# Five expert loads of each layer, asked for in three transfers of 8, 8 and 112 rows

## The reference, cut to what matters

```python
for l in range(DEPTH):                      # DEPTH = 2
    mix = _token_mixer(x, w_in[l], ..., w_out[l])
    x = _layer_norm(ALPHA * x + mix, ln1_g[l], ln1_b[l])
    ffn = _moe(x, w_router[l], b_router[l], w_gate[l], w_up[l], w_down[l], ws_gate[l], ws_up[l], ws_down[l])
    x = _layer_norm(ALPHA * x + ffn, ln2_g[l], ln2_b[l])

def expert_rows(args):                      # one of 64 experts, width 256
    xb, e = args
    h = jax.nn.silu(xb @ w_gate[e]) * (xb @ w_up[e])
    return h @ w_down[e]
```

## Time and profile before

| what | value |
|---|---|
| median of 3 runs | 1236.44 us (1235.01 to 1237.77) |
| the profiled execution, its own time | 1237.52 us |
| span of its trace, first to last instruction | 1235.7 us |
| PE busy | 1209.2 us, 98% |
| DVE, ACT, POOL busy | 560.4, 343.6, 123.8 us |
| granted clock of TensorE, mean | 0.994 |
| moved by DMA | 454.88 MB, mean 368 GB/s |

### The profile page before, as it was taken

The page is one execution under the profiler, slowest core; times in us unless marked ns, Lnnn a source line. Parts: engine busy times, 40 slices in busy tenths (PEclk is TensorE's granted clock), DMA queues, the critical chain, the costliest instruction groups (busy, mean ns, idle before and its releaser), DMA issues.

```text
span 1235.7 us, 25287 instructions
## 1 busy us (share of the span) xinstructions
PE 1209.2 (98%) x10417; PEld 631.1 (51%) x10417; DVE 560.4 (45%) x1552; ACT 343.6 (28%) x703; POOL 123.8 (10%) x173
## 2 busy tenths in 40 slices
PE   9999999999999999999999999999999999999996
PEld 8886753344344343433389868434433444443342
DVE  6888653333333333333378877433333333333334
ACT  5657411111111111111266574111111111111111
POOL 2662100000000000000035522000000000000000
PEclk9999999999999999999999999999999999999998
DMA  9554799999999999999845539999999999999994
GB/s 361 180 187 182 301 405 427 424 427 425 427 424 424 429 425 427 425 427 426 342 170 203 201 141 360 412 427 426 424 429 426 425 425 427 428 425 426 424 428 200
DMA packets 42425, 454.88 MB, mean 368 GB/s; under 512 B 4944, under 2 KB 5712, under 8 KB 8016
## 3 DMA queue, kind: packets, MB, share of 16 engines
q1 hardware_dynamic: 42032, 452.27, 88.0%
q10 hardware_dynamic: 288, 1.05, 0.2%
HBM read 452.26 MB, written 1.05 MB: 367 GB/s over the span
## 4 chain that ended last, share of the span: by engine, by line
PE 83%; DVE 9%; DMA 5%; ACT 2%; issue 1%; POOL 1%; DVEq 0%; ACTq 0%; POOLq 0%
PE banks L1078 34%; PE banks L1098 17%; PE banks L1054 7%; PE banks L1109 5%; DMA expert_weights<-in_moe_w 5%; PE banks L1086 2%; PE banks L610 1%; PE banks L998 1%; PE banks L612 1%; PE banks L611 1%; PE banks L947 1%; PE banks L1035 1%; PE banks L949 1%; PE banks L948 1%; DVE prob L1719 1%
## 5 line engine op out<-in xcount | busy, mean ns | idle before, releaser
L1078 PE MATMUL banks<-expert_weights,gathered 128*64 128x512 f32 x1520 | 341.5, 598 | 2.4 <-DMA expert_weights<-in_moe_w 2.4
L1078 PEld LDWEIGHTS banks<-expert_weights,gathered 128*64 128x64 f32 x1520 | 106.0, 137 | 232.9 <-issue 232.9
L1098 PE MATMUL banks<-expert_weights,hT 128*32 128x512 f32 x1600 | 182.0, 595 | 2.5 <-DVE hT L1926 2.5
L1921 DVE TENSOR_TENSOR sig<-sig,banks 128x256 f32<-128x256 f32 x64 | 27.0, 421 | 339.8 <-ACT sig L1451 339.5
L1464 ACT ACTIVATE y_hi<-banks,gate_slot 128x512 fp32r<-128x512 f32 x126 | 86.6, 687 | 295.1 <-PE banks L1098 295.1
L1931 DVE SCALAR_TENSOR_TENSOR y_lo<-banks,gate_slot,y_hi 128x512 fp32r<-128x512 f32 x126 | 94.7, 751 | 157.6 <-ACT y_hi L1464 157.6
L1451 ACT ACTIVATE sig<-banks 128x256 f32<-128x256 f32 x64 | 24.6, 384 | 410.5 <-PE banks L1078 410.5
L1054 PEld LDWEIGHTS banks<-hot,x_part 128*128 128x128 bf16 x3072 | 93.3, 98 | 48.7 <-issue 48.7
L1098 PEld LDWEIGHTS banks<-expert_weights,hT 128*32 128x32 f32 x1600 | 47.5, 109 | 109.4 <-issue 107.9
L1054 PE MATMUL banks<-hot,x_part 128*128 128x64 bf16 x3072 | 100.6, 193 | 0.0
L1520 POOL TENSOR_TENSOR piece_lo<-pieces,piece_hi 128x256 fp32r<-128x256 f32 x112 | 88.7, 828 | 75.3 <-ACT piece_hi L1275 61.0
(11 more groups left out here) (250 smaller groups left out, 1530.9 us busy)
## 6 DMA issues: line engine op xcount, KB each, us to landing
expert_weights<-in_moe_w SPq DMA_DIRECT2D x132, 2048.0 KB, 23.4
expert_weights_in_ring<-in_moe_w SPq DMA_DIRECT2D x20, 2048.0 KB, 23.4
pieces<-in_pieces SPq DMA_DIRECT2D x32, 1024.0 KB, 5.9
expert_weights<-in_moe_w SPq DMA_DIRECT2D x26, 1024.0 KB, 9.3
expert_weights_in_rows<-in_moe_w SPq DMA_DIRECT2D x22, 1024.0 KB, 22.5
expert_weights_in_x<-in_moe_w SPq DMA_DIRECT2D x22, 1024.0 KB, 23.3
expert_weights_in_ring<-in_moe_w SPq DMA_DIRECT2D x8, 1024.0 KB, 8.9
shared_weights<-in_ws SPq DMA_DIRECT2D x2, 3072.0 KB, 12.2
```

Source lines behind the costliest of these rows:

```text
L1078: mm = pe.matmul(C[e * PAIR:(e + 1) * PAIR, :], xgT[:, d, e * PAIR:(e + 1) * PAIR], w[e][:, part], start=(d == 0), stop=(d == KD - 1))
L1098: mm = pe.matmul((A, B)[c][to:to + SLOTS, :], hT[:, f, of_:of_ + SLOTS], W[QUARTERS + c][e][:, f * 512:(f + 1) * 512], start=(f == 0), sto ...
```

## The change

Five loads of each layer, k = 20, 36, 52, 68 and 84, are asked for in three transfers in place of one: rows 0 to 7, rows 8 to 15, and rows 16 to 127. All go into the same room, and each adds 16 to the room's semaphore, so that the counts for which PE waits take them in. All five are loads of room 4 (`expert_weights`), and none is in `IN_TWO`. What is read and where it is stored is unchanged, and no wait is added.

```diff
+LOW_ENGINES = 8
+IN_ROWS = [k for k in range(20, LOADS * PAIRS, 16)]
+assert not [k for k in IN_ROWS if k in IN_TWO]
+def rows_of(k):
+    if k not in IN_ROWS:
+        return [slice(0, P)]
+    return [slice(0, LOW_ENGINES), slice(LOW_ENGINES, 2 * LOW_ENGINES), slice(2 * LOW_ENGINES, P)]
...
-        room_ld = [sem(f"weights_loaded{r}", 16 * sum(room_of(k) == r for k in range(1, LOADS * PAIRS))) for r in range(ROOMS)]
+        room_ld = [sem(f"weights_loaded{r}", 16 * sum(len(rows_of(k)) for k in range(1, LOADS * PAIRS) if room_of(k) == r)) for r in range(ROOMS)]
...
-                return room_ld[room_of(k)], 16 * sum(room_of(m) == room_of(k) for m in before)
+                return room_ld[room_of(k)], 16 * sum(len(rows_of(m)) for m in before if room_of(m) == room_of(k))
...
                     def load(k):
-                        sp.dma_start(rooms[room_of(k)].rearrange("p j e c -> p (j e c)"), of(moe_w)[0, k // LOADS, k % LOADS]).then_inc(room_ld[room_of(k)], 16)
+                        for rows_ in rows_of(k):
+                            sp.dma_start(rooms[room_of(k)][rows_].rearrange("p j e c -> p (j e c)"), of(moe_w)[0, k // LOADS, k % LOADS, rows_]).then_inc(room_ld[room_of(k)], 16)
```

## The result

The changed kernel takes 1334.45 us (median of 4, 1329.41 to 1353.33) where the kernel before takes 1236.87 us (median of 4). The ratio is 1.0781, with a 95% interval of 1.0759 to 1.0802. I had forecast 1232.5 us, range 1231.0 to 1243.5: 98 us lost where 4 were to be won.

The account below looks back on a forecast made before the run. PE and DMA were taken to end nearly together, PE waiting only for the last pair's load; 2.06 + 1.68 + 0.33 = 4.07 us off 1236.44 gave 1232.4, put as 1232.5 us, range 1231.0 to 1243.5.

Parts of the forecast that it names:

- What bounds the kernel: PE and DMA end nearly together; PE waits only for load 94, the last pair's second gate/up half, 2.4 us in all.
- Step 1, the balance: Over five loads a layer, eight engines move 9 rows and eight 7 per load: 3.08 us more and 3.08 us less.
- The upper bound I set for the unknown form: If all eight rows of an 8-row transfer went to one engine, it would get 46 us more in a layer.
- The rule that the prediction used: On the load queue, 8-row transfers take engines 0 to 7 and the 112 rows take all 16.
- Step 2, which half is late: At a layer's end eight engines are late by 6.0 us; about two in three that the change loads the early half.
- Rival A: Late engines, or even one, take the 8-row transfers; load 94 lands 3.08 us later: 1242.6 to 1244.3 us; chance 0.26.
- The evidence I leaned on: At `in_first`, first packets start 0.95 us after issue, with late engines busy or all 16 free; called weak.
- Step 3, what PE gains: At the last pair, waits of 2.06 and 0.33 us and a clock loss of 1.68 us go: 4.07 us in sum.
- Steps 4 and 5, SP and semaphores: Ten more SP issues a layer, 0.33 to 0.40 us each, cost nothing; the extra semaphore increments take no PE time.
- B: The 8-row transfers spread over all 16 engines, so nothing shifts and PE waits as before: 1236.4 us; chance 0.07.
- C: Only part of the gain at PE's last-pair waits comes, 2.06 us or less: 1234.4 to 1236 us; chance 0.07.
- my slower rival: Rival A: late engines get extra rows, load 94 lands later in each layer, up to 1244.3 us; chance 0.26.

Follow-up runs that it names:

- slabs of 8-row transfers: Form tried against the kernel before: some columns of a load go in 16 transfers of 8 rows in steps of 4, the rest in one of 128; 1244.8 to 1267.4 us.
- the run with five slabs: Against the kernel before, all five loads send columns 0 to 511 in 16 transfers of 8 rows in steps of 4, the rest whole; 1267.4 us, ratio 1.0245.
- the two sides crossed: Against the kernel before: HBM read even/odd, SBUF written in halves side by side, 1329.8 us, 1.0758; HBM read in halves, SBUF written even/odd, 1236.1 us, 0.9999.
- one slab: Against the kernel before, load 84 alone sends columns 0 to 1279 in 16 transfers of 8 rows in steps of 4, the rest whole; 1244.8 us, ratio 1.0062.
- (two): Against the kernel before, loads 68 and 84 send columns 0 to 1279 in 16 transfers of 8 rows in steps of 4, the rest whole; 1256.3 us, 1.0153.

## Why the prediction was wrong, point by point

**What bounds the kernel.** Right. With the queues relieved of 43 us of work (the run with only rows 0 to 15) PE waits for no transfer.

**Step 1, the balance, is where it failed.** I priced a row at 0.615 us, "at 426/16 = 26.6 GB/s for an engine", whatever the rows of its transfer. That rate is one of whole loads of 128 rows. The sum had a term for how many rows each engine moves and none for which rows of SBUF the 16 engines write at one time. In its place the runs showed 1.28 us a row on average, on all 16 engines and for some 15 us, at each split load: 9.8 us a split load. The upper bound I set for the unknown form (46 us a layer if all eight rows went to one engine) comes near the loss of 49 us a layer only by chance, and lies below it; I gave it no weight. All 16 engines were busy in the slow stretches (share 1.00); none worked on alone for tens of us.

The Trainium skill had the warning, and I did not draw on it. Its page "SBUF - State Buffer", section "Door 1: The DMA port swizzle", says that a transfer's bandwidth depends on how many of SBUF's 16 ports its partitions reach, that groups of 4 rows share a port with the group 32 rows on, and that rows 0 to 63 reach eight. By it, 64 rows side by side and 16 rows in steps of 8 reach eight ports, and steps of 2 and 4 reach all 16. The runs agree on all four (224, 206, 426 and 427 GB/s in the same 12 us at load 20). With 16 rows side by side, which by the page reach four ports, the rate was 163 of 426 GB/s, lower than half but no quarter, and the time no longer than in steps of 8. Rows 16 to 127 reach all 16 ports by the page, and still they cost 8.3 us a load. So it isn't enough to reach all ports; I infer that in a whole load each engine keeps to one port, and that 7 rows for an engine break this; no run shows which port an engine writes. The page "DMA: Bandwidth & Descriptors", section "The descriptor swizzle", has such an assignment for 128 rows.

The rule that the prediction used (the Trainium skill, page "DMA: Bandwidth & Descriptors", section "Why a DMA increments its semaphore by 16 and not by 1"), by which eight rows go to the eight lowest-numbered engines, fits the runs in its count: with slabs of 8-row transfers 14 engines were left at work, then eight or two. That these are the lowest-numbered no row shows.

**Step 2, which half is late.** By the fit above it failed as well, hidden under the first. I asked which of two halves is late, and it is not a half by number: by the fit above, two of the eight late engines are among those that take the 8-row transfers. Rival A had the words, "even one of them", and 0.26. With a form that lost nothing, load 94 would then still have landed 3.08 us later and the time have been A's 1242.6 to 1244.3; no run shows this, since no form tried shifts rows at full rate. The evidence I leaned on, the first packets 0.95 us after the issue in both cases, holds for six early engines as well as for eight.

**Step 3, what PE gains.** It agrees in size, as far as the noise lets one say. I had 4.07 us as all there was to win; the run in which PE waits for no transfer is 0.9968 of the kernel before, which is 4.0 us less (interval 2.1 to 5.8); by the medians, 1233.45 and 1235.45, it is 2.0.

**Steps 4 and 5, SP and semaphores.** Right for the change: three transfers with all 128 rows in each (cut by columns) lose about 0.2 us a load. For more transfers the price of 0.33 to 0.40 us an issue is too low: in the run with five slabs, load 20 with its 17 issues and the two loads behind it took SP 12.7 us, 0.67 us an issue:

```profile
220.88 12.70 SPq L511 DMA_DIRECT2D expert_weights<-in_moe_w  x19
```

**Rivals.** B and C did not happen. What happened was on no list: my slower rival went up to 1244.3, and the range ended at 1243.5.

**Open.** What sets the length of a stretch, since bad forms as different as 2 of 64, 8 of 16 and 16 + 112 rows all lose 8.5 to 10 us a load. Why a slab loses rate (348 GB/s for 20 us), though its 8 rows go in steps of 4; writes of the low engines into rows 64 to 127 are the suspect, not tested by themselves. That the instruction queue makes the eight late remains an inference. No version that brings all the rows beat the kernel before; one that loads just the six early engines was not tried.

## What to carry to other kernels

When the DMA engines are the bound, a transfer's rows of SBUF are part of its price: keep all 128, or cut by columns or in steps of 2 or 4 that reach over all 128, and don't move rows between engines by a form that the profile has never shown at full rate. Read the DMA share and the rate together: a share of 1.0 at half the GB/s went here with the rows of SBUF that were written, and no balance of bytes can see it. I read it as engines in each other's way; the runs do not show that. And before moving work from late engines to early ones, find which engines the new form uses; "half" in a share is a number of engines, not a range of them.

## What the runs showed of the hardware that I had not expected

- In the stream of whole loads at 426 GB/s, a 2 MB load written as rows 0 to 15 and 16 to 127, as two halves side by side, or as eight transfers of 16 rows costs 8.5 to 10 us more; the same load in steps of 2 or 4 rows, or cut by columns, costs at most about 0.2 us.
- Behind a load split into 8, 8 and 112 rows the rate of the 16 engines together falls, over some 15 us, to 204 GB/s at a share of 1.00.
- Where HBM is read made no difference (1.0758 and 0.9999 with the two sides crossed).
- Eight engines finish 6.0 us behind the other eight at a layer's end, and if the steps of 3.5, 3.0, 3.0 us (one slab) and 6.9, 6.2 us (two) are read rightly, two of these eight are among the eight that an 8-row transfer uses.
